# A two-layer hybrid diffusion block: input tiles in a new order with twelve of them cut to the latent tokens, HGRN query scaling on VectorE, and the output projection in 256-token segments with its weights rounded by GpSimd

## The reference

```python
for layer in range(DEPTH):
    with_ctx = layer < DEPTH - 1
    ...
    h_l = modulate(rms_norm(x_l, norm_pre_mix[layer]), mod_l[0], mod_l[1])
    h_c = modulate(rms_norm(x_c, norm_pre_mix[layer]), mod_c[0], mod_c[1])
    o_c, o_l = token_mixing(h_c, h_l, w_in[layer], w_out[layer], ..., with_ctx)
    x_l = x_l + mod_l[2] * rms_norm(o_l, norm_post_mix[layer])
    f_l = conv_ffn(modulate(rms_norm(x_l, norm_pre_ffn[layer]), mod_l[3], mod_l[4]),
                   ffn_w_up[layer], ffn_conv_w[layer], ffn_conv_b[layer], ffn_w_down[layer])
    x_l = x_l + mod_l[5] * rms_norm(f_l, norm_post_ffn[layer])
    if with_ctx:
        x_c = x_c + mod_c[2] * rms_norm(o_c, norm_post_mix[layer])
        ...
```

## Time and profile before

| | us |
|---|---|
| median of 3 runs | 4998.82 |
| lowest, highest | 4993.88, 4999.63 |
| profiled execution | 5010.07 |
| its span | 5008.2 |
| busy in the span: PE, PEld | 3947.0 (79%), 3185.4 (64%) |
| busy in the span: DVE, ACT, POOL | 2091.9 (42%), 1449.4 (29%), 1153.9 (23%) |
| mean granted clock of TensorE | 0.891 |

### The profile page before, as it was taken

One profiled execution on the slowest core, in us unless ns is written; L12 is line 12 of the kernel. 1 busy time (PEld: TensorE's weight loads), 2 busy tenths in 40 slices (PEclk: granted clock), 3 DMA queues, 4 the chain that ended last, 5 costly groups with the idle time before them and its releaser, 6 DMA issues. The chain is left out here.

```text
span 5008.2 us, 81764 instructions
## 1 busy us (share of the span) xinstructions
PE 3947.0 (79%) x33402; PEld 3185.4 (64%) x33402; DVE 2091.9 (42%) x2830; ACT 1449.4 (29%) x1925; POOL 1153.9 (23%) x924
## 2 busy tenths in 40 slices
PE   1999449676877999999982999449658868999994
PEld 1888325455755888788771888325437757777783
DVE  6444534465546332322326222525465544232224
ACT  3111433234345312212114111433243354222221
POOL 1000720203510322323221000620205402333331
PEclk7999669787988999999996999669779989999997
DMA  3444110100012111111001333110100022111112
GB/s 130 165 157 155 44 57 1 37 3 34 4 46 76 50 35 34 34 39 34 30 26 59 119 118 123 49 55 1 37 34 4 5 75 76 47 42 46 50 42 84
DMA packets 68208, 282.62 MB, mean 56 GB/s; under 512 B 6992, under 2 KB 10320, under 8 KB 63312
## 3 DMA queue, kind: packets, MB, share of 16 engines
q1 hardware_dynamic: 52080, 196.93, 11.7%
q10 hardware_dynamic: 15840, 81.53, 4.5%
HBM read 221.55 MB, written 49.02 MB: 54 GB/s over the span
## 5 line engine op out<-in xcount | busy, mean ns | idle before, releaser
L3388 POOL TENSOR_TENSOR wu_raw_rest<-wu_raw,wu_hi 128x1024 fp32r<-128x1024 f32 x88 | 215.3, 2446 | 1414.6 <-POOLq L3387 1414.6
L3356 DVE SCALAR_TENSOR_TENSOR y<-ps,taps,y 128x1023 f32<-128x1023 f32 (+1 forms) x132 | 134.1, 1016 | 870.2 <-DVEq L3354 863.7
L451 PE MATMUL ps<-h_hi,wu_hi 128*128 128x512 f32 x1680 | 460.2, 371 | 12.6 <-PEq L3267 12.6
L451 PE MATMUL ps<-h_whole_rest,wu_hi 128*128 128x512 f32 x1680 | 459.0, 371 | 0.0
L451 PE MATMUL ps<-h_hi,wu_raw_rest 128*128 128x512 f32 x1680 | 459.0, 371 | 0.0
L451 PE MATMUL ps<-h_hi,w_hi 128*128 128x512 f32 x1296 | 327.6, 361 | 84.5 <-PEq L447 84.5
L3380 DVE TENSOR_TENSOR xT<-ps,xT 128x1280 f32<-128x1280 f32 (+1 forms) x160 | 217.2, 1358 | 312.5 <-DVEq L3373 312.5
L451 PEld LDWEIGHTS ps<-h_hi,wu_hi 128*128 128x128 f32 x1680 | 294.6, 188 | 69.8 <-issue 13.8
L451 PEld LDWEIGHTS ps<-h_hi,wu_raw_rest 128*128 128x128 f32 x1680 | 294.1, 188 | 56.4
L451 PEld LDWEIGHTS ps<-h_whole_rest,wu_hi 128*128 128x128 f32 x1680 | 294.2, 188 | 56.1
L451 PE MATMUL ps<-h_hi,w_raw_rest 128*128 128x512 f32 x1296 | 326.1, 360 | 0.0
(11 more groups left out here) (330 smaller groups left out, 7704.7 us busy)
## 6 DMA issues: line engine op xcount, KB each, us to landing
wu_raw<-in_w_up_dram SPq DMA_DIRECT2D x88, 512.0 KB, 3.3
rows<-rows ACTq DMA_DIRECT2D x54, 640.0 KB, 4.8
w_raw<-in_w_in_dram SPq DMA_DIRECT2D x54, 512.0 KB, 4.4
ada_w<-in_ada_rest_dram ACTq DMA_DIRECT2D x27, 1024.0 KB, 7.2
wd_raw<-in_w_down_dram SPq DMA_DIRECT2D x44, 512.0 KB, 4.3
raw<-rows SPq DMA_DIRECT2D x24, 640.0 KB, 4.4
ada_w<-in_ada_rest_dram ACTq DMA_DIRECT2D x27, 512.0 KB, 5.0
h_whole<-rows SPq DMA_DIRECT2D x20, 640.0 KB, 6.3
```

What stands on the lines that cost most here:

```text
L451: mm = pe.matmul(ps[:, lo:lo + width], w[a][:, t, :], rhs[b][:, t, lo:lo + width], start=(t == 0 and i == 0), stop=(t == n_k - 1 and i == 2))
L3356: dve.scalar_tensor_tensor(y[:, s, lo + 1:hi], ps[s][:, lo:hi - 1], k.taps[:, s, 0:1], y[:, s, lo + 1:hi], ALU.mult, ALU.add).then_inc(own ...
L3388: pool.tensor_tensor(wu_lo[:, s], wu_raw[:, s], wu_hi[:, s].bitcast(F32), ALU.subtract)\
```

## The change

Three parts.

1. Input projection, both layers: the 27 tiles are in another order (the weights are permuted on their way in, and every reader of a tile goes by the new numbers). Tiles 0 to 13 hold what the context gives to others: HGRN's gates and values, the attentions' keys and values, DeltaNet's keys and values. Tiles 14 to 25 hold queries and output gates. In layer 1 these twelve are multiplied, evicted and stored for the 1024 latent tokens alone. TensorE's and ScalarE's loop becomes two, 7 pairs and 6 pairs. In layer 0 all have 1280 tokens.
2. HGRN heads, both layers: VectorE scales the queries of all levels (`scale_queries`), in halves g ahead of each merge; GpSimd keeps the keys and `tot`. TensorE's level l waits for `queries_scaled` instead of GpSimd's step.
3. Output projection, both layers: segments (512, 256, 256, 256) in layer 0; layer 1 keeps (512, 256, 256). GpSimd rounds `w_out`'s tiles and the first two of `w_up` (a copy with a change of type), VectorE keeps `w_out`'s remainders. The four weight slots are now one of `w_up`'s, two of `w_down`'s and one new, so that `w_up`'s first tile is loaded early (with load 5) and rounded after the eighth weight. Layer 0 has 20 loads instead of 16. The first norm's steps of segment s-1 and the second norm's of s-2 run side by side, two tiles at each p = 1 to 4, their factors together at p = 0 (`factors`). Behind the last segment, VectorE interleaves the first norm of the last segment with the second norm of the one before it.

```diff
-T_GDN, T_Z, T_BQ, T_BK, T_BV, T_CQ, T_CK, T_CV, T_HQ, T_HF, T_HI, T_HG, T_BETA = (
-    0, 6, 8, 10, 11, 12, 14, 15, 16, 18, 22, 24, 26)
+T_HF, T_HI, T_BK, T_BV, T_CK, T_CV, T_GK, T_GV, T_GQ, T_Z, T_BQ, T_CQ, T_HQ, T_HG, T_BETA = (
+    0, 4, 6, 7, 8, 9, 10, 12, 14, 16, 18, 20, 22, 24, 26)
+T_GDN = (T_GQ, T_GQ + 1, T_GK, T_GK + 1, T_GV, T_GV + 1)
+TILE_ORDER = (18, 19, 20, 21, 22, 23, 10, 11, 14, 15, 2, 3, 4, 5, 0, 1, 6, 7, 8, 9, 12, 13, 16, 17, 24, 25, 26)
...
+        n_own = SEQ if layer == DEPTH - 1 else T
+        whole_pairs = T_GQ // 2
...
-            act.activation(out[:, s, :], ps[s][:, 0:T], ACT.Copy).then_inc(own_a, 1)
+            act.activation(out[:, s, 0:n], ps[s][:, 0:n], ACT.Copy).then_inc(own_a, 1)
...
-            act.dma_start(k.rows[tile], out[:, s, :]).then_inc(out_free[s], 16)
+            act.dma_start(k.rows[tile][:, 0:n], out[:, s, 0:n]).then_inc(out_free[s], 16)
...
+                with pe.Fori(0, whole_pairs) as i:
+                    multiply(pe, 1, T)
+                    multiply(pe, 0, T)
+                with pe.Fori(0, pairs - whole_pairs) as i:
+                    multiply(pe, 1, n_own)
+                    multiply(pe, 0, n_own)
...
+                def scale_queries(a, l, g):
...
+                    wait_products(dve, a, l, g)
+                    if l == 0:
+                        dve.wait_ge(started.sem, started.at(a + 1))
+                    else:
+                        dve.wait_ge(tots_done.sem, tots_done.at(6 * a + l))
+                        dve.wait_ge(queries_scaled.sem, queries_scaled.at(scaled_before(a, l, g)))
                     for d in both:
-                        ends = f[:, 2 * d + a, :].rearrange("q (c m x) -> q c m x", x=2, c=chunks)
-                        late = side(queries_of(a, d)[:, first:last], 0, 1 - d)
-                        ins = dve.tensor_tensor(late, late, ends[:, first:last, :, d:d + 1], ALU.mult)
-                    ins.then_inc(first_scaled.sem, 1)
+                        ends = (f[:, 2 * d + a, :] if l == 0 else tots[a][d][l - 1][:, :])\
+                            .rearrange("q (c m x) -> q c m x", x=2, c=chunks)
+                        late = side(queries_of(a, d)[:, first:last], l, 1 - d)
+                        ins = dve.tensor_tensor(late, late, ends[:, first:last, :, d:d + 1].to_broadcast(
+                            [P, last - first, HD >> (l + 1), 1 << l]), ALU.mult)
+                    ins.then_inc(queries_scaled.sem, 1)
...
-                        else:
-                            first_scale(a, g)
+                        scale_queries(a, l, g)
...
                     merge(0, l)
+                for g in both:
+                    scale_queries(0, PAIRS - 1, g)
                 merge(1, 0)
...
-                    if l:
-                        wait_products(pool, a, l, g)
-                        for d in both:
-                            late = side(queries_of(a, d)[:, first:wanted], l, 1 - d)
-                            ins = pool.tensor_tensor(late, late, ends[d][:, first:wanted, :, d:d + 1].to_broadcast(
-                                [P, wanted - first, HD >> (l + 1), 1 << l]), ALU.mult)
...
-                        if l == 1:
-                            pe.wait_ge(first_scaled.sem, first_scaled.at(2 * a + g + 1))
+                        if l:
+                            pe.wait_ge(queries_scaled.sem, queries_scaled.at(scaled_before(a, l, g)))
...
+    def factors(self, act, s):
+        if s >= 1:
+            self.ln1(act, s - 1)
+        if s >= 2:
+            self.ln2(act, s - 2)
+        if s >= 1:
+            self.exp1(act, s - 1)
+        if s >= 2:
+            self.exp2(act, s - 2)
...
-        segs = ((0, 512), (512, 512), (1024, 256)) if n > SEQ else ((0, 512), (512, 256), (768, 256))
+        segs = [(0, 512)] + [(lo, 256) for lo in range(512, n, 256)]
+        last = len(segs) - 1
...
-        w_raw, w_hi, w_lo = ([u[:, 0], u[:, 1]] + [d[:, q, :].rearrange(by_tile, m=P) for q in range(2)]
-                             for u, d in ((wu_raw, wd_raw), (wu_hi, wd_hi), (wu_lo, wd_lo)))
...
+        w_raw, w_hi, w_lo = ([u[:, 1]] + [d[:, q, :].rearrange(by_tile, m=P) for q in range(2)] + [m[:, :, :]]
+                             for u, d, m in ((wu_raw, wd_raw, more_raw), (wu_hi, wd_hi, w_more), (wu_lo, wd_lo, more_lo)))
...
+                if g == last - 1:
+                    ref.sum2(pe, last)
                 for s in range(2):
+                    if g == 0:
+                        pe.wait_ge(wu_pe[s], 1)
+                        pe.sem_inc(wu_pe[s], -1)
+
+                        pe.wait_ge(ps_free[s], 1)
+                        pe.sem_inc(ps_free[s], -1)
...
+                    if j >= 12 and j % 4 == 0:
+                        spill(j // 4 - 3)
...
+                    if j == 5:
+                        sp.dma_start(wu_raw[:, 0], a["w_up"][layer, 0]).then_inc(wu_in[0], 16)
+                sp.wait_ge(out_done.sem, out_done.at(end - 3))
+                sp.dma_start(wu_raw[:, 1], a["w_up"][layer, KF]).then_inc(wu_in[1], 16)
...
+                    if s >= 2 and p == 0:
+                        ref.sum2(pe, s - 2)
                     if s and p == 0:
                         ref.sum1(pe, s - 1)
-                    if s and p == 5:
...
-                def round_w(j):
-                    q = loads[j][0] % 4
-                    act.wait_ge(w_in[q].sem, w_in[q].at(16 * nth_in(j)))
-                    act.activation(w_hi[q], w_raw[q], ACT.Copy).then_inc(w_hi_done.sem, 1)
...
+                    if p == 0:
+                        ref.factors(act, s)
+                    if 1 <= p <= 4:
+                        for u in (2 * p - 2, 2 * p - 1):
+                            if s >= 1:
...
-                        if p == 5:
-                            ref.factor2(act, s - 1)
...
+                            if s >= 2:
+                                ref.upper(act, s - 2, u)
...
+                    if i + 3 in fresh:
+                        rest_w(fresh[i + 3])
+                    if s and p == 1:
+                        dve.wait_ge(evicted.sem, evicted.at(8 * s))
+                        dve.wait_ge(out_done.sem, out_done.at(8 * s))
+                    if 1 <= p <= 4:
+                        group = (2 * p - 2, 2 * p - 1)
+                        if s >= 1:
                             for u in group:
                                 ref.scale_y(dve, s - 1, u)
                             for u in group:
                                 ref.add_x(dve, s - 1, u)
-                        if p in (1, 2, 3, 4):
...
+                        if s >= 2:
+                            for u in group:
+                                ref.scale_x(dve, s - 2, u)
+                    if s >= 1 and 1 <= p <= 5:
+                        for u in range(max(2 * p - 3, 0), min(2 * p - 1, KD)):
+                            ref.add2(dve, s - 1, u)
+                    if s >= 2 and 1 <= p <= 5:
+                        for u in range(max(2 * p - 3, 0), min(2 * p - 1, KD)):
+                            ref.lower(dve, s - 2, u)
...
+                for u in range(KD + 2):
+                    if u < KD:
+                        ref.scale_y(dve, last, u)
+                        ref.scale_x(dve, last - 1, u)
+                    if 1 <= u <= KD:
+                        ref.add_x(dve, last, u - 1)
+                        ref.lower(dve, last - 1, u - 1)
+                    if u >= 2:
+                        ref.add2(dve, last, u - 2)
...
+                def weights(j):
+                    q = loads[j][0] % 4
+                    pool.wait_ge(w_in[q].sem, w_in[q].at(16 * nth_in(j)))
+                    pool.tensor_copy(w_hi[q], w_raw[q]).then_inc(w_hi_done.sem, 1)
...
+                    pool.tensor_copy(wu_hi[:, s], wu_raw[:, s]).then_inc(own["pool"], 1)
...
+                for j in range(len(loads)):
+                    weights(j)
+                    if j == 7:
+                        first_up(0)
+                first_up(1)
...
-        ins.append(tiles(np.concatenate([qkv_z, rest, last], 1), KD))
+        ins.append(tiles(np.concatenate([qkv_z, rest, last], 1), KD)[list(TILE_ORDER)])
```

197 lines of the change are left out of this document (82 added, 115 removed).

## The result

The changed kernel takes 4945.87 us (median of 4 runs, 4942.34 to 4948.15) against 4996.35 (4 runs, 4993.51 to 4999.63): 50.5 us less, ratio 0.9898 with a 95% interval of 0.9881 to 0.9915. Forecast were 79 us less, 4920 with a range of 4892 to 4948. The direction and the range hold, the range by 2 us, which is less than the runs of one kernel scatter. The size was two thirds of what was forecast, and nearly all of the missing 28 us lies in part 3: the output projections and their tails.

What follows compares the result with a forecast made beforehand. TensorE was taken to bound layer 1's projection, GpSimd to lead in HGRN, and no engine to be full in the output projection. Terms -38 - 10 - 14 - 17 = -79 us gave 4920 us, range 4892 to 4948.

Steps and rivals of the forecast that it cites:

- The tiles: Layer 1's input projection: twelve tiles of 1024 columns take 10.9 us instead of 14.06; -38 us, bounds -34 to -40.
- HGRN: HGRN heads: with queries scaled on VectorE a level takes 4.6 us against 6.1; -5 us a layer, -10 for both.
- The pair of scalings: HGRN on VectorE: two query scalings taken at 1.4 us, between 0.9 and 2.28; sign of success 0.9 to 1.6.
- The segments' idle time: Output projection, layer 0: VectorE's waits for the norm's factors, 3.2, 4.4 and 2.4 us, within 94 us for three segments.
- The tail: Last output-projection eviction to first ConvFFN tap: 31 us in both layers, -11 us in layer 0 and -2 in layer 1.
- The rounding on GpSimd: Output projection: one weight rounding on GpSimd takes 1.2 us; sign of success 1.0 to 1.4.
- Two signs of being wrong: VectorE's 0.42 us operations at 1 us and more beside GpSimd's roundings; any unlisted stage moving by over 5 us.
- B: Rival: VectorE takes it all back, parts 2 and 3 give nothing, -38 is left, 4961 us; chance 0.12.
- C: Rival: more than forecast, HGRN -28, layer 0 -22, layer 1 -27, tiles -38, so 4884 us; chance 0.12.
- D: Rival: slower, each GpSimd operation holds VectorE for its own whole length, +19, 5018 us; chance 0.04.
- E: Rival: the tiles don't get faster because the next weight comes too late, -41 is left, 4958 us; chance 0.02.
- The sum: Whole kernel: tiles -38, HGRN -10, layer 0's output projection and tail -14, layer 1's -17; together -79 us.

Runs made afterwards that it cites:

- e1: Kernel before with only the new tile order and the twelve tiles without context in layer 1; ratio to before 0.9921 (0.9908 to 0.9934).
- e2: Kernel before with only the HGRN change, query scaling of all levels on VectorE; ratio to before 0.9978 (0.9969 to 0.9987).
- e5: Changed kernel with the output weights rounded by ScalarE again, GpSimd keeping only the first two up tiles; ratio to before 0.9896 (0.988 to 0.9913).
- e7: Kernel before with only layer 0's output projection in segments of 512, 256, 256, 256, old list of operations; ratio to before 1.0031 (1.002 to 1.0042).
- e12: Kernel of e6 with layer 0's output projection back in segments of 512, 512, 256, both up tiles loaded at the end; ratio to before 0.9863.
- e6: Changed kernel with ScalarE's split put ahead of the last segment's square behind the last segment; 4930.23 us, ratio to before 0.9859.

## Why the prediction was right, and where it was not

**The tiles**: -38 forecast, -38.4 in the trace and -39 in e1 (whose interval reaches from -33 to -46). TensorE was the bound, the helper's pitch for two pieces was in the trace, and the slack of the weights held.

**HGRN**: -10 forecast, -11 in e2. The pair of scalings was taken at 1.4 us; 48 instructions take 32.6 us in layer 0, 1.36 a pair, alone 0.82 and beside GpSimd up to 2.13, a wider spread than the 0.9 to 1.6 that was given as a sign:

```profile
529.14 2.13 DVE L2254 TENSOR_TENSOR qp<-qp,tot 128x320 f32<-128x320 f32 x2
...
555.68 0.82 DVE L2254 TENSOR_TENSOR qp<-qp,tot 128x320 f32<-128x320 f32 x2
```

These are the two ends of the earlier trace rows, and the value between them was right. Here the two engines did hold each other, and the move paid all the same, since GpSimd had led by 21 us. The Trainium skill ("Perfetto Trace Analysis", section Optimizing Scalar/DVE Operations) warns that moving work between these two might not help, since they share an SBUF read port. A hold between them is in these rows (2.13 us against 0.82), and e2 shows that the exchange helped all the same. The split between the layers was not right: layer 1's part is 3.4 in nearly every trace, layer 0's 4 to 8, against 5 and 5 forecast.

**The segments' idle time.** This is the step that failed: "3.2 in which VectorE has to wait for the factor", 4.4 and 2.4 for the next two. These 10 us were 5.7, 7.3 and 6.2 at the boundaries themselves, and with the shorter waits between them VectorE is idle for 24.7 of the 109.1 us from the last eviction of the first segment to that of the last. Its work was counted rightly: busy for 84.4 us against 80 counted and 4 added for contention. The contention is real; without GpSimd's roundings of `w_out` VectorE is busy for 79.7 us (e5). Longest held was a pair of the second norm's beside GpSimd's remainder of a `w_up` tile, 3.00 us against 0.88 for another pair. So 109 us came where 94 were taken. Against the table's +7.4 and -3 the miss is only 10, because the 97 us that were taken for before left out 4.8 of the 101.8 that the same two segments took.

The kernel before had the size of that wait in its own trace: 8.48 us at 1522.37, and 5.73 at 4089.87, where the next tile has 256 tokens as it has now in layer 0. The forecast took 3.2. In layer 1, with no new boundary, the same step failed: idle 16.8 us where 3.2 + 3.2 + 1.6 were counted, busy 57.1 against 58.6. That left -9.9 of -15. TensorE's granted clock in layer 1's segments rose from 0.84 to 0.91 at the same time, and its share in the -9.9 is not separated.

The sign of layer 0 comes from the additional segment, which costs 16 us by itself under the old list (e7). Most of that is VectorE's work in shorter pieces, which the forecast had counted; what it did not ask is what the same cut saves, and e12 shows that three segments are as fast.

**The tail**: 31 us forecast, 40.1 and 40.0 measured. TensorE's wait of 12.7 us did go. But the rounds were counted by VectorE's own operations, 1.9 us, without asking what the split that each round needs stands behind in ScalarE's queue. They took 2.5 to 2.8, and e6 shows that it was this: with the swap the rounds are 1.5 to 1.9 and the tails 30.3 and 32.3 us, about the forecast's number. (The forecast's mark, the end of the last square, lies 0.6 us behind the table's.) The two tails are 16 of the missing 28 us.

**The rounding on GpSimd** was taken at 1.2. Of the 36, 19 last 1.04 us and the others up to 1.97, beyond the 1.0 to 1.4 that was given as a sign. It pays off no more than ScalarE's and costs no more (e5).

**Two signs of being wrong came.** Nine of VectorE's 256-column operations in the output projections and their tails, which take 0.42 to 0.49 us alone, took 1.07 to 2.60. They belong to the contention above, which the forecast had priced, and not to what it missed. And a stage off the list, layer 0's attention, moved by 10.0 us. The second profile of before has 7.7 of them, so most of it is no part of the change.

**The rivals.** B (VectorE takes everything back, 4961) is half of what came: for part 3 it is right in size, but by the waits at the boundaries and a queue, and by contention only in a small part; for part 2 it is wrong. C's larger gains are nowhere but in e6's tail. D and E are out. The sum -38 - 10 - 14 - 17 became -38 - 11 + 5 - 4.
